# Half of an output projection in three fp32r terms, and the first experts' products in another order

## The reference, cut to what matters

```python
y = jnp.concatenate([rms_norm(o_sb, g_out_sb), rms_norm(o_rg, g_out_rg), rms_norm(o_ca, g_out_ca)], axis=-1)
return y @ w_out                       # (256 x 1024) @ (1024 x 1024), added to x
...
hid = jax.nn.silu(t @ wg) * (t @ wu)   # per expert: 1024 -> 256
return acc + g[:, None] * (hid @ wd)   # 256 -> 1024, for all 64 experts
```

## Time and profile before

| | us |
|---|---|
| median of three executions | 583.2 |
| the profiled execution | 584.03 |
| its span, from the first to the last instruction | 582.3 |
| TensorE busy (matmul) | 552.1 (95%) |
| TensorE weight load busy, beside the matmuls | 307.3 (53%) |
| VectorE busy | 209.3 (36%) |
| ScalarE busy | 159.5 (27%) |
| GpSimd busy | 24.2 (4%) |
| moved by DMA | 227.5 MB, 391 GB/s over the span |

### The profile page before, as it was taken

The page is one execution under the profiler, slowest core; times in us unless marked ns, Lnnn a source line. Parts: engine busy times, 40 slices in busy tenths (PEclk is TensorE's granted clock), DMA queues, the critical chain, the costliest instruction groups (busy, mean ns, idle before and its releaser), DMA issues.

```text
span 582.3 us, 8347 instructions
## 1 busy us (share of the span) xinstructions
PE 552.1 (95%) x3164; PEld 307.3 (53%) x3165; DVE 209.3 (36%) x533; ACT 159.5 (27%) x308; POOL 24.2 (4%) x78
## 2 busy tenths in 40 slices
PE   8999999999999999999999989999999989689975
PEld 6988875466444445555455544544544444245332
DVE  2889798684325222220222221111222221221113
ACT  5787366343111122220222221122111212121102
POOL 1006231100000000000000000000000000000000
PEclk9999999999999999999999999999999999898999
DMA  8997469968999999999999999999999999999994
GB/s 318 419 420 298 186 271 424 345 241 314 383 382 423 423 420 421 429 424 423 425 425 424 429 419 426 427 424 426 426 422 427 433 420 427 422 425 424 423 409 184
DMA packets 27929, 227.51 MB, mean 391 GB/s; under 512 B 3312, under 2 KB 3440, under 8 KB 7792
## 3 DMA queue, kind: packets, MB, share of 16 engines
q1 hardware_dynamic: 27600, 226.67, 94.3%
q10 hardware_dynamic: 288, 0.29, 0.1%
HBM read 225.90 MB, written 1.05 MB: 390 GB/s over the span
## 4 chain that ended last, share of the span: by engine, by line
PE 71%; DMA 21%; SPq 4%; DVE 3%; issue 1%; ACT 0%
PE ps L1771 27%; DMA cell_two<-in_w_e 14%; PE ps L1800 10%; PE ps L1729 7%; PE ps L1829 5%; PE ps L1636 5%; DMA cell_three<-in_w_e 4%; PE ps L1532 4%; PE ps L1499 3%; SPq L586 2%; DMA cell_d<-in_w_e 2%; PE ps L1513 2%; SPq L580 1%; PE ps L1791 1%; PE ps L1521 1%
## 5 line engine op out<-in xcount | busy, mean ns | idle before, releaser
L1771 PE MATMUL ps<-cell_two,xg 128*64 128x512 f32 (+2 forms) x624 | 123.5, 611 | 13.1 <-DMA cell_two<-in_w_e 11.4
L1800 PE MATMUL ps<-cell_d,e_hT 128*64 128x512 f32 (+2 forms) x488 | 93.4, 597 | 2.7 <-DVE e_hT L1391 2.7
L1771 PEld LDWEIGHTS ps<-cell_two,xg 128*64 128x64 f32 (+2 forms) x624 | 41.0, 131 | 93.4 <-issue 93.4
L1771 PE MATMUL ps<-cell_gu,xg 128*64 128x512 f32 (+2 forms) x416 | 78.6, 595 | 1.9 <-DMA cell_gu<-in_w_e 1.8
L1388 DVE TENSOR_TENSOR e_h<-e_sg,ps 128x256 f32<-128x256 f32 x28 | 11.8, 421 | 182.2 <-ACT e_sg L906 182.2
L906 ACT ACTIVATE e_sg<-ps 128x256 f32<-128x256 f32 x28 | 10.7, 384 | 204.0 <-PE ps L1771 204.0
L1456 DVE SCALAR_TENSOR_TENSOR ylo<-ps,gslot,yhi 128x512 fp32r<-128x512 f32 (+1 forms) x53 | 39.2, 740 | 73.8 <-ACT yhi L917 73.8
L1729 PE MATMUL ps<-pick,xhi 128*128 128x256 f32 x224 | 58.5, 300 | 0.3 <-DVE pick L1304 0.3
L917 ACT ACTIVATE yhi<-ps,gslot 128x512 fp32r<-128x512 f32 (+1 forms) x53 | 35.9, 679 | 71.6 <-PE ps L1800 70.2
L1729 PE MATMUL ps<-pick,xlo 128*128 128x256 f32 x224 | 54.3, 281 | 0.0
L1729 PEld LDWEIGHTS ps<-pick,xhi 128*128 128x128 f32 x224 | 42.3, 189 | 19.8 <-issue 19.7
(11 more groups left out here) (342 smaller groups left out, 639.0 us busy)
## 6 DMA issues: line engine op xcount, KB each, us to landing
cell_two<-in_w_e SPq DMA_DIRECT2D x39, 2048.0 KB, 28.7
cell_d<-in_w_e SPq DMA_DIRECT2D x59, 1024.0 KB, 26.4
cell_gu<-in_w_e SPq DMA_DIRECT2D x48, 1024.0 KB, 18.6
wo<-in_w_out SPq DMA_DIRECT2D x1, 4096.0 KB, 12.5
wA<-in_w_qk SPq DMA_DIRECT2D x7, 512.0 KB, 10.8
wR<-in_w_rest SPq DMA_DIRECT2D x3, 1024.0 KB, 28.4
cell_three<-in_w_e SPq DMA_DIRECT2D x1, 3072.0 KB, 24.4
wV<-in_w_v SPq DMA_DIRECT2D x1, 2048.0 KB, 18.6
```

What stands on the lines that cost most here:

```text
L1771: last = mm(ps[side * w:(side + 1) * w, U, :], rows(k, slice(side * w, (side + 1) * w)), weight[:, k - k0, :], start=k == 0, stop=k == KD - 1)
L1800: last = mm(ps[side * w:(side + 1) * w, Y[half], :], e_hT[:, kk, side * w:(side + 1) * w], n[:, kk, half * 512:(half + 1) * 512], start=kk ...
```

## The change

The projections of RG and CA (chunks 4 to 7) are computed as three fp32r terms in place of one fp32 product; those of attention stay fp32. For that, ScalarE copies the four weight chunks into `wo_hi` (a new tile over cells 9 and 10), GpSimd writes `wo_lo` in place over the upper half of `wo`, ScalarE's gain step writes `yT_hi`, and VectorE writes `yT_lo`. On TensorE group 0 ends before its down products; group 1 does its gate and up products first, then the down products of group 0, then its own. The hidden rows of group 0 get a tile of their own, `e_hT0`. The fixed loads and the first cells are put in another order, and the planner counts the down cells of group 0 as freed later. Some small tiles move (`gslot`), and an unused semaphore goes.

```diff
+    freed_at = dict(used_at)
+    for e in groups[0].experts:
+        freed_at["down", e] = (1, 1.5)
...
-    first_cells = [16, 4, 17, 5, 3, CELLS, 1, 6, 2, 7, 8, 9, 10, 11, 18, 12, 13, 14, 20, 0, 19, 15]
+    first_cells = [16, 4, 17, 5, 3, CELLS, 1, 6, 2, 7, 0, 8, 11, 20, 18, 12, 14, 9, 13, 10, 19, 15]
...
+    wo_hi = at("wo_hi", o_ring + 72 * KB, [P, KD // 2, D], F32R)
+    wo_lo = at("wo_lo", o_A + 16 * KB, [P, KD // 2, D], F32R)
...
             sp.wait_ge(o_ps, SB_HEADS)
-            load_shared("high")
             load_fixed("low", 3)
             load_fixed("high", 3)
+            load_fixed("down", 3)
 
             sp.wait_ge(unit_ps, 20)
             load_fixed("low", 4)
             load_fixed("high", 4)
-            load_fixed("down", 3)
             load_fixed("down", 4)
             load_fixed("low", 5)
-            load_fixed("low", 6)
             sp.wait_ge(unit_ps, 33)
             ...
             load_fixed("high", 5)
             sp.wait_ge(yrg_dve, 2)
-            load_fixed("down", 6)
+            load_fixed("down", 5)
             sp.wait_ge(wo_ps, 4)
-            load_shared("low")
+            load_fixed("low", 6)
             sp.wait_ge(unit_ps, 35)
             load_fixed("down", 2)
             sp.wait_ge(wo_ps, 10)
             load_fixed("high", 6)
+            load_fixed("down", 6)
             sp.wait_ge(wo_ps, len(projections))
-            load_fixed("down", 5)
+            load_shared("low")
+            load_shared("high")
...
+            def projection_low(k):                                     # GpSimd
+
+                pool.wait_ge(whi_act, len(splits) + k + 1)
+                pool.tensor_tensor(wo_lo[:, k, :], wo[:, KD // 2 + k, :], wo_hi[:, k, :].bitcast(F32),
+                                   ALU.subtract).then_inc(wo_lo_pool, 1)
+
+            projection_low(0)
+            projection_low(1)
+            projection_low(2)
             pool.wait_ge(unit_ps, 26)
             for k in (4, 6):
+                if k == 6:
+                    projection_low(3)
                 pool.wait_ge(ysq_act, k + 2)
                 pool.tensor_tensor(y_sq[:, k, :], y_sq[:, k, :], y_sq[:, k + 1, :], ALU.add).then_inc(ysum_pool, 1)
...
+            def projection_high(k):                                    # ScalarE
+
+                act.wait_ge(wo_loaded, 16)
+                act.wait_ge(unit_ps, 14)
+                nc.scalar.copy(wo_hi[:, k, :], wo[:, KD // 2 + k, :]).then_inc(whi_act, 1)
...
                     nc.scalar.copy(wT[n % 2][:], ps[:, 6, 0:NZ]).then_inc(wT_act, 1)
+                    if n == SB_HEADS - 2:
+                        projection_high(0)
+                        projection_high(1)
...
+            group_root(0)
+            projection_high(2)
+            projection_high(3)
+            for i in range(2):
+                act.wait_ge(yrg_dve, i + 1)
+                square_and_gain(4 + i)
+            act.wait_ge(oca_dve, 1)
+            square_and_gain(6)
+            group_root(1)
+            act.wait_ge(oca_dve, 2)
+            square_and_gain(7)
+            group_root(2)
...
+            def rows_low(k):                                           # VectorE
+
+                dve.wait_ge(yg_act, k + 1)
+                nc.vector.scalar_tensor_tensor(yT_lo[:, k - KD // 2, :], yT[:, k, :], vec[:, GOUT + k:GOUT + k + 1],
+                                               yT_hi[:, k - KD // 2, :].bitcast(F32), ALU.mult, ALU.subtract).then_inc(alo_dve, 1)
+
             ca_evac(2)
             ca_evac(3)
+            rows_low(4)
+            rows_low(5)
             ca_result(0)
...
             mean_square(1, RG)
+            rows_low(6)
+            rows_low(7)
             residual(4)
...
+                    for m, (y, w) in enumerate(((yT_hi, wo_hi), (yT_hi, wo_lo), (yT_lo, wo_hi))):   # TensorE
+                        last = mm(ps[:, ACC[2 * t + half], :], y[:, k - KD // 2, rows], w[:, k - KD // 2, c],
+                                  start=k == chunks[0] and m == 0, stop=k == chunks[-1] and m == 2)
...
+            def first_down():
+
+                for e in groups[0].experts:
+                    wait_loaded(pe, "down", e)
+                pe.wait_ge(hTs_dve, 1)
+                for half in range(2):
+                    copied(pe, 1, half)
+                    down([weights("down", e) for e in groups[0].experts], y_ps, (half,), rows=e_hT0)
...
+                if g.index == 1:
+                    first_down()
...
                 hidden_T(e_h, hT_ps)
+                if g.index == 1:
+                    pe.wait_ge(S_act, 1)
+                    for half in range(2):
+                        pe.wait_ge(yhi_act, half + 1)
+                        pe.wait_ge(ylo_dve, half + 1)
+                        scatter(S, halves=(half,))
```

More of the change, by code:

```diff
@@ L138, in last_use @@
     def last_use(cells):
-        return sorted((used_at[held[i]] for i in cells), reverse=True)
+        return sorted((freed_at[held[i]] for i in cells), reverse=True)
     def take(part, e, cells):
@@ L151, in hybrid_decoder_layer @@
             two = min(neighbours, key=lambda ab: last_use(ab)[0])
-            one = min((i for i in held if i not in two), key=lambda i: used_at[held[i]])
+            one = min((i for i in held if i not in two), key=lambda i: freed_at[held[i]])
             if max(last_use(two + (one,))) < last_use(three)[0]:
@@ L158, in hybrid_decoder_layer @@
             take(part, e, three)
-            used_at["low", e] = used_at["high", e] = used_at["down", e]
+            freed_at["low", e] = freed_at["high", e] = freed_at["down", e]
         elif part == "both":
@@ L162, in hybrid_decoder_layer @@
         else:
-            take(part, e, (min(held, key=lambda i: used_at[held[i]]),))
+            take(part, e, (min(held, key=lambda i: freed_at[held[i]]),))
         later.append((part, e))
@@ L1632, in project @@
                 chunks = ((0, 1, 2, 3), (4, 5), (6, 7))[g]
+                rows, c = slice(t * P, (t + 1) * P), slice(half * 512, (half + 1) * 512)
                 for k in part or chunks:
-                    if t == 0 and half == 0:
+                    if t == 0 and half == 0 and not g:
                         pe.wait_ge(yg_act, k + 1)
-                    last = mm(ps[:, ACC[2 * t + half], :], yT[:, k, t * P:(t + 1) * P],
-                              wo[:, k, half * 512:(half + 1) * 512], start=k == chunks[0], stop=k == chunks[-1])
+                    if t == 0 and half == 0 and g:
+                        pe.wait_ge(alo_dve, 1 + KD + k + 1 - KD // 2)
+                        pe.wait_ge(wo_lo_pool, k + 1 - KD // 2)
+                    if not g:
+                        last = mm(ps[:, ACC[2 * t + half], :], yT[:, k, rows], wo[:, k, c],
+                                  start=k == chunks[0], stop=k == chunks[-1])
+                        continue
+                    for m, (y, w) in enumerate(((yT_hi, wo_hi), (yT_hi, wo_lo), (yT_lo, wo_hi))):
+                        last = mm(ps[:, ACC[2 * t + half], :], y[:, k - KD // 2, rows], w[:, k - KD // 2, c],
+                                  start=k == chunks[0] and m == 0, stop=k == chunks[-1] and m == 2)
                 if k == chunks[-1]:
@@ L1793, in shared_down, with down @@
                     last.then_inc(sem, 1)
-            def down(cells, sem, halves=range(2), kks=range(KH)):
+            def down(cells, sem, halves=range(2), kks=range(KH), rows=e_hT):
                 w = P // len(cells)
@@ L1799, in down @@
                         for side, n in enumerate(cells):
-                            last = mm(ps[side * w:(side + 1) * w, Y[half], :], e_hT[:, kk, side * w:(side + 1) * w],
+                            last = mm(ps[side * w:(side + 1) * w, Y[half], :], rows[:, kk, side * w:(side + 1) * w],
                                       n[:, kk, half * 512:(half + 1) * 512], start=kk == 0, stop=kk == KH - 1,
@@ L1954, in group @@
                 cells = [weights("down", e) for e in g.experts]
-                if g.index == 0:
-                    for half in range(2):
-                        copied(pe, 1, half)
-                        down(cells, y_ps, (half,))
-                    return
                 for step in g.steps:
```

52 lines of the change are left out of this document (31 added, 21 removed).

## The result

The changed kernel takes **591.74 us** (median of 6 runs, 589.36 to 594.46) against 583.52 for the kernel before, run beside it: 8.2 us more, ratio **1.0134 [1.0113, 1.0156]**. The forecast was 585.0, with a range up to 588.3. Its sign was right, its size too small by 6.7 us. The profiled execution took 594.46, its span is 592.7. One execution of the kernel before took 632.82 us, far above the other five, and the ratios of this document leave such slow executions out.

The account below looks back on a forecast made before the run. Bound: the last byte's arrival, bytes over 424 GB/s plus DMA shortfall before about 182 us. Ranking +2.5, groups -0.35, about 0.3 regained: +1.9 on the 583.2 median, 585.1, said as 585.0; range 580.2 to 588.3.

Parts of the forecast that it names:

- The hole in the DMA stream at 101: Fixed loads end near 101, leaving some 6 us (8 with the lock); 2 MB refill the 124 to 134 hole; cost zero.
- ScalarE's copies: Four 128x1024 weight copies, 1.07 us each, fit idle time before 80.86 and 101.45; cost zero, 2.1 us if uncovered.
- The lock: GpSimd and VectorE exclude each other on the shared SBUF port for whole instructions; as walked 585.0, chance 0.50.
- the walk of GpSimd's part: Four 2.36 us subtractions delay VectorE at normalisation, recurrence and last pair addition; project(6) 4 us late, ranking 2.5 later.
- rival (b): Harder lock: 128x2 scalings behind the cross-attention maxima wait too; ranking about 5 us late, 588.1; chance 0.12.
- The saving: RG and CA projections: three fp32r terms save 0.186 us 16 times, 2.97 us; about 1.5 reach the ranking without waits.
- The four `rows_low`: VectorE's low parts of the rows, 128x256 each: 1.5 to 1.9 us in all, absorbed in gaps between residuals.
- The groups: Groups 0 and 1 reordered: group 1's down products end 0.35 us earlier, since TensorE skips the wait for hidden rows.

Follow-up runs that it names:

- the fp32 run: Changed kernel with the RG and CA projections back in fp32, without copies, subtractions or rows_low; loads and groups as changed: 583.63 us, ratio 0.9987.
- the run without low weight: Changed kernel without GpSimd's four subtractions; TensorE's second term multiplies the rows' low part with the weight's high part again: 583.48 us, ratio 0.9985.
- the run with the last two as memsets: Changed kernel with the subtractions of chunks 6 and 7 replaced by memsets, those of 4 and 5 whole: 587.14 us, ratio 1.0062.
- the run with dummies: Changed kernel with ten dummy fp32 products of 128x256 in TensorE's three stalls: ratio 1.0111 [1.0093, 1.0129].

## Why the prediction was wrong

**What held.** The end moved by what the ranking moved: in the changed kernel 8.2 us both, and in every run with the same routing the median, less that of the kernel before beside it, is within 1.8 us of the shift of the ranked load. Between 182 and 560 nothing changed. The hole in the DMA stream at 101 was refilled (20.7 of 20.8 MB in the fp32 run), cost zero as said. ScalarE's copies were hidden: two of 1.00 us with 0.82 us of idle time left behind them, two with 2.45 (in the run without low weight, where nothing delayed VectorE). A subtraction took 2.33 against 2.36. The lock is there in both directions.

**The step that failed: the walk of GpSimd's part.** It let VectorE wait only where its instructions were large and "SBUF to SBUF": 1.7 at the normalisation, 1.7 in the recurrence, and it made project(6) 4 us late. Four waits came, 7.47 us, and project(6) came 7.9 late (118.06 - 88.73 against 109.77 - 88.36). With that the ranking was 8.2 late and not 2.5. Three sizes were wrong.

- The two scalings of 128x2 waited, 1.84 + 1.51. This was rival (b), given 0.12 on the ground that such small instructions may stay off the port. The runs show that being small is no protection: 0.17 us of work waited 1.84. The waits at the normalisation, which the forecast had instead, did not occur, because VectorE got there at 95.79, after the second subtraction.
- The recurrence waited 2.04, not 1.7. The third subtraction began at 101.24 and not near 98, because ScalarE's copy had slipped with the scalings, and the product waited to its end.
- The pair `rows_low(4)` and `(5)` waited 2.08 for the fourth subtraction. The walk had that subtraction meet only the last pair addition and `rows_low(6)`. But whoever is pushed back meets the next subtraction: the same delay that moved `rows_low` put it beside the fourth one.

Rival (b) had the first of these waits at about 4 us, where the runs show 3.35 (alone in the run with the last two as memsets, 587.14). But it took only about 1 us for the later two, which came to 4.12, and so ended at 588.1. The walks are also loose by tenths: the evacuations "near 106.7" are 106.4 by their own terms, and (b) says 5 us and adds 5.2.

**The saving.** 2.97 us on paper and 1.5 in the walk; without any wait 0.86 reached the ranking. A product took 0.237 us at full clock (4.27 / 18) and not 0.229, which leaves 2.6 on paper. The four `rows_low` took 2.4 us in all, not 1.5 to 1.9, and were absorbed as said: in the run without low weight project(4) starts 17.39 from the pair addition, as before. The last projection ended 1.28 earlier (120.29 - 88.88 against 121.05 - 88.36); the next 0.4 went in what stands between it and the ranking, which I did not follow.

**The clock.** The prediction had no term for it. In the profiled execution two stretches ran at 0.50 behind the stalls:

```profile
98.00:101.30 3.30, 3.30 (x5) 1.28 (x4) 3.23 (x11) 3.27 (x7) 0.06 (x1) 0.50 1.04 432
118.40:121.60 3.20, 3.20 (x9) 2.48 (x8) 1.14 (x3) 0.00 (x0) 0.00 (x0) 0.50 1.01 425
```

That is the lower of the two levels, 1.2 GHz. The first was covered by VectorE's wait for the third subtraction (in the run with dummies, at full clock there, TensorE stood 1.29 us for it ahead of the last cross-attention product), the second cost 1.56. So 7.47 - 0.86 + 1.56 = 8.17 against the measured 8.18 at the ranking.

**The groups.** The forecast gave them 0.35. From the first ranked load to the end of group 1's down products it is 172.41 - 144.03 = 28.38 after and 163.84 - 135.48 = 28.36 before: nothing. The premise that TensorE no longer stands for group 0's hidden rows was wrong: each group still begins with a wait for the hidden rows of the one before (`hTs_dve`, L1969 of the changed kernel), so group 1's products don't follow the slot table at once.

```profile
155.13 7.09 PE L1840 MATMUL ps<-cell_gu,xg 128*64 128x512 f32 x32 [0.18 <-DVE e_hT L1448]
```

The two stops of before were 0.38 and 0.27 us. Now this one is 0.18, and a new one of 0.37 came in the middle of the first scatter, at 167.32, for group 0's result, which is made right before it.

**Rule and measurement.** The Trainium skill, SBUF — State Buffer, section Who interferes with whom, has all of it but the prices: instructions with one tensor from SBUF that use both ports contend with any GpSimd instruction, those with two SBUF inputs with one that reads, and all others with none. The traces agree with it (scaling beside memsets 1.48 against 0.17; product beside a memset 0.69, as alone; residual beside a subtraction 0.75, as alone). By this rule, which sets no least size, rival (b) deserved the chance that the forecast had.

## What to carry to other kernels

Before work goes to GpSimd, list every VectorE instruction that stands beside it by its operands, not by its size, and let each wait to the end of the GpSimd instruction; then do it again with the delayed times, since what is pushed back meets the next one. In these runs work on GpSimd was free beside VectorE instructions that read PSUM, and, where it only wrote, beside those with two inputs in SBUF. On a chain without gaps such waits add up one to one, and a fall of TensorE's clock can come on top.

## What the runs showed of the hardware

- A VectorE scaling of 128x2, 0.17 us, took 2.01 beside a GpSimd subtraction of 2.33 and 1.48 beside memsets of 0.92. Cutting the GpSimd work to 0.69 us pieces made each wait at most 0.57, and more of them.
- GpSimd waits for VectorE as well: a pair addition of 0.73 took 2.62.
- From the ranked load's issue to the end of the span it was 444.6 to 449.3 us in the 15 traces of kernels with the same routing. The four longest, 448.3 and more, are those in which the last 32 gate and up products took 6.4 to 6.6 us; where they took 3.64, at full clock, it was 444.6 to 447.1. So one execution cannot tell 1 us at the end. The place of the ranked load can tell 0.1: it was 47.12 and 47.11 in two kernels without waits, 53.74 in two with the same ones.
